# Eight query tiles of an input projection multiplied as four pairs of seven products, and decoding that begins behind them

## The chip, the cores and the metric

The kernel runs on one core of a Trainium2 chip. The metric is the device time of one launch in microseconds, the median of several runs. A profiled execution gives the rows below; its span runs from the first to the last instruction of the core.

## What is computed

One layer of a decoder step for a prompt of 512 tokens and 8 sample tokens of eight other sequences, which share one pass (520 columns, `TOK`). The hidden size is 2048. Cut to its core:

```python
h = rms_norm(x)
z = h @ w_in                       # 2048 x 7168, fp32; columns qd kd vd gd qw kw vw gw qm gm
od = differential_attention(qd, kd, vd)   # 4 heads, two 128-wide q/k halves each, value 256
ow = dilated_window_attention(qw, kw, vw) # 4 heads of 128
mk, mv = rms_norm(mem) @ w_mem_kv         # 256 memory tokens
om = attention(qm, mk, mv)                # 4 heads of 128
y = x + concat(rms(od) * silu(gd), ow * silu(gw), om * silu(gm)) @ w_out
return rms_norm(y), new keys and values
```

The sample tokens attend to caches: per sequence 1024 past keys and values of the differential heads in pages of 128 (a page table names them), a window cache and 256 memory keys and values. This is "decoding" below.

## The kernel before

**Tiles.** The output features are cut into tiles of 128 (`tiles`, L108): 8 of the memory projection (`mk`, `mv`), then 56 of the input projection: `qd` (8: head and half), per head `kd`, `vd`, `gd` (two each), `qm` (4), `qw` (4), `kw` (4), `vw`/`gw` (8), `gm` (4), and last the output projection `y`. A tile is computed transposed: the weight block is stationary, the 520 token columns move, as two halves of 260 (`HALF`) into two banks of PSUM tensor `z[0]` or `z[1]`, in turn by unit. fp32 products are made of three passes: weights and tokens are both split into a high part (`w_hi`, `act_hi`, fp32r) and a low rest (`w_lo`, `act_lo`), and hi*hi, hi*lo, lo*hi are summed. ScalarE makes `w_hi` (`split_hi`, L1351), VectorE `w_lo` (`split_lo`, L1676).

**Slots.** All engines run through one list `PLAN` of slots. A slot holds one operation on TensorE: a quarter of a single tile (`quarter`, L1097: 4 row blocks x 3 passes x 2 column halves = 24 matmuls), or half a product of a pair (`product`, L1123: 12 matmuls). Splits are made three slots ahead (`AHEAD`) in a ring of four (`SPLIT_RING`); raw weights come by SyncE's queue, 256 KB each, into a ring of eight (`WIN_RING`, L828). Behind its operation a slot has jobs that every engine does in a fixed order of rank: evacuations, turning transposes, attention steps and decoding.

**Pairs.** Ten of the sixteen `y` tiles are computed in five pairs: two tiles and the whole of the tokens make a 2x2 block product (rows of weights `A`, columns and depth of tokens `B`), with seven products in place of eight (`PRODUCTS`). It needs sums of weights (`weight_sum`, L1692 to L1700, eight a pair), sums of products (`part_copy` on ScalarE, `part_out` on VectorE, L1714 to L1729), and four operands T1 to T4 made once of the right-hand side (`operand_add`, four subtractions of 260 columns per row block; `operand_hi`, L1430 and `operand_lo`, L1757, each over 1040 columns). The operands lie in `arena`, the memory that keys, gates, pages and attention buffers use before; the raw sums lie in the places of T3's and T4's parts until these are split.

**Attention** steps (`att_steps`) come in the order scores on TensorE (A), row maximum on VectorE (`step_max`, L1797, L1804), exponential on ScalarE, normalised probabilities on VectorE (`step_probs`, L1822), turning (L1183), values, and for differential heads `o_nat` scaled on VectorE behind GpSimd's reciprocal root (L1829) and turned (L1210), gated into `cat`. Per differential head four steps, six slots apart (four in the last head).

**Decoding.** Query rows of the samples are stored to DRAM and read back broadcast (`qrows`, `q_bc`). Then 320 page units, 160 of keys (four multiply-and-add reductions each, L1865) and 160 of values (L1892, L1894), are placed in slots by the planner. It gives each slot a room of 1.5 x its length less VectorE's planned load, sums the rooms between `first` and `end`, and fills the slots in proportion:

```python
first, end = DONE[AT["qd", 1, 1]] + 4, DONE[AT["gw", 3, 0]] - 2
room = [max(0.3, 1.5 * span[s] - load[s]) for s in range(n_slots)]
```

Pages are loaded by SyncE's queue up to three slots ahead into a ring of six (`PAGE_RING`). `IN_START` is slot 32, `IN_END` slot 256. Behind the last input tile `cat` is complete, is split into `act_hi` and `act_lo` (L1596, L2144), and then its space is used for the residual (`nat`, L981).

## Time and profile before

| | |
|---|---|
| time, median of 3 runs | 1026.35 us (1026.08 to 1027.72) |
| the profiled execution | 1026.25 us |
| its span | 1024.5 us |
| TensorE matmuls busy | 98% of the span |
| weight loads busy | 96% |
| VectorE busy | 71% |
| ScalarE busy | 43% |
| GpSimd busy | 5% |
| from HBM and to it | 197 GB/s over the span |
| granted TensorE clock | 0.997 of full |

Busy shares are means over stages with different limits: preparation of tokens (to about 75 us), query tiles without decoding (to about 133), input tiles with attention and decoding (to about 771), the last input tiles, and the output projection. An engine's line in the rows gives the source line of this kernel.

### The profile page before, as it was taken

What the parts mean: (1) busy time and instruction counts of PE and PEld (TensorE: products, weight loads), DVE (VectorE), ACT (ScalarE), POOL (GpSimd) and SP (SyncE); (2) the same over time, 40 slices, a digit from 0 to 9 for tenths busy, and PEclk for the clock granted to TensorE, in tenths of its full rate; (3) what the DMA queues carried; (4) which work ended last, traced back from release to release, by engine and by line L of the source; (5) the groups of instructions that cost most, each with busy time, mean ns of one, the idle gap of its engine ahead of it and who ended that gap; (6) DMA issues with size and microseconds to landing.
All of it is one profiled execution on the core that took longest, in us unless ns stands there. A gap on an engine that the chain in (4) does not pass through costs nothing.

```text
span 1024.5 us, 24055 instructions
## 1 busy us (share of the span) xinstructions
PE 1000.5 (98%) x8103; PEld 980.4 (96%) x8103; DVE 723.7 (71%) x2687; ACT 441.5 (43%) x1169; POOL 54.7 (5%) x122
## 2 busy tenths in 40 slices
PE   7999999999999999999999999999999999999995
PEld 6899999999999999999999999999999999999995
DVE  5783267777788867778777676577774786588874
ACT  5763222222333333444342553335565365545552
POOL 0200000000000000000000000000000100000002
PEclk9999999999999999999999999999999999999998
DMA  9863288987978877777866686999662425234424
GB/s 300 250 195 107 64 266 265 293 271 226 266 220 254 259 231 235 219 224 207 245 200 192 186 249 181 231 280 284 193 191 72 140 74 153 94 104 145 124 84 167
DMA packets 254521, 203.33 MB, mean 198 GB/s; under 512 B 12480, under 2 KB 207670, under 8 KB 253750
## 3 DMA queue, kind: packets, MB, share of 16 engines
q1 hardware_dynamic: 253934, 200.67, 65.7%
q8 instruction: 65, 1.06, 0.4%
q10 hardware_dynamic: 464, 1.12, 0.3%
q14 instruction: 58, 0.48, 0.1%
HBM read 189.98 MB, written 11.76 MB: 197 GB/s over the span
## 4 chain that ended last, share of the span: by engine, by line
PE 91%; DVE 2%; ACT 2%; issue 2%; SPq 1%; DMA 1%; POOL 0%; DVEq 0%; POOLq 0%; ACTq 0%
PE z L1097 71%; PE z L1123 8%; PE o_ps L1193 2%; PE s_ps L1156 2%; PE t_ps L1143 2%; PE t_ps L1183 1%; PE s_ps L1161 1%; DMA w_raw<-in_w_mem_kv_dram 1%; PE o_ps L1198 1%; PE o_ps L1202 1%; PE s_ps L1168 1%; PE o_ps L1242 1%; ACT w_hi L1351 1%; PE s_ps L1028 1%; SPq L828 1%
## 5 line engine op out<-in xcount | busy, mean ns | idle before, releaser
L1097 PE MATMUL z<-act_hi,w_hi 128*128 128x260 f32 (+1 forms) x2048 | 440.9, 291 | 2.4 <-DVE act_lo L1629 2.3
L1097 PE MATMUL z<-act_hi,w_lo 128*128 128x260 f32 (+1 forms) x2048 | 422.4, 283 | 0.0
L1097 PE MATMUL z<-act_lo,w_hi 128*128 128x260 f32 (+1 forms) x2048 | 421.6, 282 | 0.0
L1097 PEld LDWEIGHTS z<-act_hi,w_hi 128*128 128x128 f32 x2048 | 321.5, 189 | 7.9 <-issue 4.0
L1097 PEld LDWEIGHTS z<-act_lo,w_hi 128*128 128x128 f32 x2048 | 319.9, 188 | 0.0
L1097 PEld LDWEIGHTS z<-act_hi,w_lo 128*128 128x128 f32 x2048 | 319.5, 188 | 0.0
L1676 DVE TENSOR_TENSOR w_lo<-w_raw,w_hi 128x512 fp32r<-128x512 f32 x302 | 206.8, 687 | 132.5 <-ACT w_hi L1351 131.8
L1351 ACT ACTIVATE w_hi<-w_raw 128x512 fp32r<-128x512 f32 x302 | 186.4, 626 | 200.4 <-PE z L1097 173.2
L1865 DVE CUSTOM_DVE_ANT_0 pages<-pages,q_bc 128x128 f32<-128x128 f32 x640 | 144.2, 285 | 21.2 <-DMA pages<-in_cache_k_win_dram 13.5
L1894 DVE SCALAR_TENSOR_TENSOR v_acc<-pages,dec_a,v_acc 128x256 f32<-128x256 f32 x224 | 94.3, 478 | 1.7 <-DMA pages<-in_cache_v_diff_dram 1.5
L1473 ACT ACTIVATE probs<-probs,st_n 128x128 f32<-128x128 f32 (+3 forms) x48 | 26.8, 558 | 79.9 <-DVE st_n L1804 79.6
L1865 DVE DVE_READ_ACCUMULATOR2_ANT dec_s<- 128x1 f32 x640 | 51.6, 81 | 0.0
L1491 ACT ACTIVATE probs_T<-t_ps 128x512 f32<-128x512 f32 (+3 forms) x40 | 18.8, 470 | 68.4 <-PE t_ps L1183 55.8
L1797 DVE CUSTOM_DVE_ANT_0 probs<-s_ps,bias 128x128 f32<-128x128 f32 (+3 forms) x48 | 22.3, 490 | 35.3 <-PE s_ps L1156 22.7
L1123 PE MATMUL z<-t_hi,w_hi 128*128 128x260 f32 x160 | 45.8, 286 | 0.0
L1123 PE MATMUL z<-t_hi,w_lo 128*128 128x260 f32 x160 | 45.2, 282 | 0.0
L1123 PE MATMUL z<-t_lo,w_hi 128*128 128x260 f32 x160 | 45.1, 282 | 0.0
L1351 ACT ACTIVATE w_hi<-w_sum 128x512 fp32r<-128x512 f32 x40 | 25.2, 629 | 34.2 <-DVE w_sum L1700 12.9
L1676 DVE TENSOR_TENSOR w_lo<-w_sum,w_hi 128x512 fp32r<-128x512 f32 x40 | 27.5, 687 | 14.9 <-ACT w_hi L1351 14.9
L1123 PE MATMUL z<-act_hi,w_hi 128*128 128x260 f32 x120 | 34.8, 290 | 0.5 <-DVE w_lo L1676 0.4
L1123 PE MATMUL z<-act_lo,w_hi 128*128 128x260 f32 x120 | 33.9, 282 | 0.0
L1123 PE MATMUL z<-act_hi,w_lo 128*128 128x260 f32 x120 | 33.9, 282 | 0.0
(236 smaller groups left out, 1121.8 us busy)
## 6 DMA issues: line engine op xcount, KB each, us to landing
w_raw<-in_w_in_dram SPq DMA_DIRECT2D x224, 256.0 KB, 4.5
pages<-in_cache_k_diff_dram SPq DMA_DIRECT2D x128, 256.0 KB, 4.7
pages<-in_cache_v_diff_dram SPq DMA_DIRECT2D x128, 256.0 KB, 3.6
w_raw<-in_w_out_dram SPq DMA_DIRECT2D x64, 256.0 KB, 2.8
w_raw<-in_w_mem_kv_dram SPq DMA_DIRECT2D x32, 256.0 KB, 6.1
cat<-in_x_prompt_dram SPq DMA_DIRECT2D x8, 1024.0 KB, 6.0
q_bc<-q_rows_dram SPq DMA_DIRECT2D x32, 256.0 KB, 6.7
pages<-in_cache_mem_k_dram SPq DMA_DIRECT2D x16, 256.0 KB, 6.4
```

The lines of the kernel that those rows point to most:

```text
L1097: last = nc.tensor.matmul(zb[:, bank, 0:b - a], lhs[:, w], rhs[:, kt, a:b], start=(kt == 0 and m == 0), stop=(kt == KT - 1 and m == 2))
L1123: last = nc.tensor.matmul(out, lhs[:, w], rhs[:, j, :], start=(i == 0 and j == 0 and m == 0), stop=(i == 1 and j == 3 and m == 2))
L1143: last = nc.tensor.transpose(t_ps[:, b * P:(b + 1) * P], src[:, b * P:(b + 1) * P], ident[:, :])
L1156: last = nc.tensor.matmul(s_ps[:, c, 0:(i + 1) * P], cat_t[:, 2 * h + c, i * P:(i + 1) * P], kT_t[:, key_slot("kd", h, c), 0:(i + 1) * P], ...
L1193: last = nc.tensor.matmul(o_ps[:, 0:2 * P], probs_T[:, kb * P:(kb + 1) * P], v_nat[:, h % 2, kb, :], start=(kb == 0), stop=(kb == i))
L1351: nc.scalar.activation(hi, raw, ACT.Copy).then_inc(s_hi, 1)
L1473: last = nc.scalar.activation(probs[:, c, 0:w], src, ACT.Exp, bias=st_n[:, t % 2, c:c + 1], scale=SCALE, accum_out=st_l[:, t % 2, c:c + 1])
L1491: nc.scalar.activation(probs_T[:, 0:w], t_ps[:, 0:w], ACT.Copy).then_inc(s_tfree, 1)
L1676: nc.vector.tensor_tensor(lo, raw, hi.bitcast(F32), ALU.subtract).then_inc(s_lo, 1)
L1797: last = nc.vector.tensor_tensor_reduce(probs[:, c, 0:w], s_ps[:, c, 0:w], bias[:, bi % 2, SEQ - w:SEQ], 1.0, LOWEST, ALU.add, ALU.max, st ...
L1865: last = nc.vector.tensor_tensor_reduce(seg, seg, q_bc[:, i % 2, k * P:(k + 1) * P], 1.0, 0.0, ALU.mult, ALU.add, s3[:, t, col:col + 1])
L1894: last = nc.vector.scalar_tensor_tensor(acc[:, seg], pages[:, slot, seg], a, acc[:, seg], ALU.mult, ALU.add)
```

## The change

The order of input tiles becomes: four `qm` tiles, each single as before; then the eight `qd` tiles as four pairs by the seven products; then everything else as before, without the `qm` tiles in the middle. `FIRST_QM = 4` takes all of them.

- The right-hand side of these pairs is the normalised tokens. They exist only as high and low parts, so `token_sum` adds them into `x_full` (16 additions of 520 columns), and `operand_add`, `operand_hi` and `operand_lo` make T1 to T4 of it during the `qm` tiles (`X_SUM_AT`, `X_ADD_AT`, `X_SPLIT_AT`). The same functions make the second set for the output pairs, now wholly behind `IN_END` (`T_ADDS`, `T_SPLIT_AT`).
- The parts of a query pair go straight into the query rows of `cat`.
- The operands lie in `arena` and the weight sums in the memory of the kept sample columns. So the bias tables, the kept query columns (`keep_first`), the query rows and the first pages wait for `Q_END`, the end of the fourth pair. Pages may be planned from `Q_END + 4` to two slots behind the last `gw` tile.
- Weight loads for the pairs are issued one slot behind the freeing of their place, in place of four.

`IN_END` becomes 280. Cut diff (renamed waits of equal meaning left out):

```diff
...
+FIRST_QM = 4
...
-    out += [("qd", h, c) for h in range(H) for c in range(2)]
+    out += [("qm", j, 0) for j in range(FIRST_QM)] + [("qd", h, c) for h in range(H) for c in range(2)]
...
-    out += [("qm", j, 0) for j in range(H)] + [("qw", j, 0) for j in range(H)] + [("kw", j, 0) for j in range(H)]
+    out += [("qm", j, 0) for j in range(FIRST_QM, H)] + [("qw", j, 0) for j in range(H)] + [("kw", j, 0) for j in range(H)]
...
-FIRST_IN = AT["qd", 0, 0]
+FIRST_IN = 2 * H
...
-        paired = kind == "y" and c == 0 and FIRST_PAIRED <= e <= LAST_PAIRED
+        paired = kind == "qd" or kind == "y" and c == 0 and FIRST_PAIRED <= e <= LAST_PAIRED
...
+Q_PAIRS = H
+Q_END = START[PAIRS_OF_TILES[Q_PAIRS - 1]] + 14
...
-            loads.append((n, r, slot, used[slot], event, at + (1 if first >= IN_END else AHEAD + 1)))
+            loads.append((n, r, slot, used[slot], event, at + (1 if first >= IN_END or IN_START + 8 <= first < Q_END else AHEAD + 1)))
...
-T_ADDS = ((2, -11), (0, -10), (1, -9), (4, -8), (5, -7), (3, -4), (6, 1), (7, 1))
+T_ADDS = ((2, 1), (0, 1), (1, 2), (4, 2), (5, 3), (3, 3), (6, 4), (7, 4))
 T_SPLITS = ((2, 0), (1, 0), (2, 1), (1, 1), (3, 0), (3, 1), (4, 0), (4, 1))
-T_SPLIT_AT = (-4, 2, 2, 3, 4, 4, 6, 8)
+T_SPLIT_AT = (5, 6, 7, 8, 9, 10, 11, 12)
 HEADS_AT = ((0, 1, 2, 3), (4, 5, 6, 7), (8, 9, 10, 11), (12, 13, 14), (15,))
-RESIDUAL_AT = (3, 20, 46, 74)
+RESIDUAL_AT = (5, 20, 46, 74)
+X_SUM_AT = tuple(IN_START + 1 + j // 2 for j in range(HALF_KT))
+X_ADD_AT = tuple(IN_START + 5 + 3 * j // 4 for j in range(HALF_KT))
+X_SPLIT_AT = tuple(IN_START + 11 + j for j in range(HALF_KT))
...
-    put(DONE[AT["qd", 1, 1]] + 1, "qrows", 0)
-    put(DONE[AT["qd", 3, 1]] + 1, "qrows", 1)
-    put(DONE[AT["qm", 3, 0]] + 1, "qrows", 2)
+    put(Q_END + 1, "qrows", 0)
+    put(Q_END + 2, "qrows", 1)
+    put(max(Q_END + 6, DONE[AT["qm", 3, 0]] + 1), "qrows", 2)
...
-    queries = {0: AT["qd", 1, 1], 1: AT["qd", 3, 1], WINDOW: AT["qw", 3, 0], MEMORY: AT["qm", 3, 0]}
+    ready = {0: Q_END + 4, 1: Q_END + 5, WINDOW: DONE[AT["qw", 3, 0]] + 4, MEMORY: max(Q_END + 9, DONE[AT["qm", 3, 0]] + 4)}
...
-    first, end = DONE[AT["qd", 1, 1]] + 4, DONE[AT["gw", 3, 0]] - 2
+    first, end = Q_END + 4, DONE[AT["gw", 3, 0]] + 2
...
-    assert STEPS[-1][3] + 3 < IN_END - 4 and fin0 + 5 < IN_END - 10
+    assert STEPS[-1][3] + 3 < IN_END - 4 and fin0 + 5 < IN_END - 4
     for j, (kt, turn) in enumerate(T_ADDS):
-        put(IN_END + turn, "T", ("add", j))
+        put(X_SUM_AT[j], "T", ("sum", j))
+        put(X_ADD_AT[j], "T", ("add", j))
+        put(IN_END + turn, "T", ("add", HALF_KT + j))
     for j in range(len(T_SPLITS)):
-        put(IN_END + T_SPLIT_AT[j], "T", ("split", j))
+        put(X_SPLIT_AT[j], "T", ("split", j))
+        put(IN_END + T_SPLIT_AT[j], "T", ("split", len(T_SPLITS) + j))
...
+        x_full = nc.alloc_sbuf_tensor_at("x_full", [P, HALF_KT, 2, TOK], F32, offset=base)
...
-                if s in (30, 31):
-                    bias_table(s - 30)
+                if s in (Q_END + 1, Q_END + 2):
+                    if s == Q_END + 1:
+                        sp.wait_ge(s_quarter, Q_END)
+                    bias_table(s - Q_END - 1)
...
-                        sp.wait_ge(s_tadd, len(T_ADDS))
+                        sp.wait_ge(s_tadd, 2 * len(T_ADDS))
...
-                    if k == 0:
-                        pe.wait_ge(s_tlo, T_SPLITS.index((t, i)) + 1)
+                    if k in (0, Q_PAIRS):
+                        pe.wait_ge(s_tlo, len(T_SPLITS) * (k // Q_PAIRS) + T_SPLITS.index((t, i)) + 1)
...
-                if k == 0:
-                    act.wait_ge(s_kout, 16 * len(NAT_K))
-                else:
+                if k in (0, Q_PAIRS):
+                    act.wait_ge(s_kout, 16 * (H if k == 0 else len(NAT_K)))
+                if k:
...
-                t, half = T_SPLITS[j]
-                if j == 0:
+                again, i = divmod(j, len(T_SPLITS))
+                t, half = T_SPLITS[i]
+                if j == len(T_SPLITS):
...
-                act.wait_ge(s_tadd, T_ADDED[half])
+                act.wait_ge(s_tadd, HALF_KT + T_ADDED[half] if again else HALF_KT)
                 if t >= 3:
-                    act.wait_ge(s_tlo, T_SPLITS.index((t - 2 if t == 3 else 2, half)) + 1)
+                    act.wait_ge(s_tlo, len(T_SPLITS) * again + T_SPLITS.index((t - 2 if t == 3 else 2, half)) + 1)
...
+                    if i == H:
+                        act.wait_ge(s_pdve, 7 * Q_PAIRS)
...
+                below, above = slice(0, HALF), slice(HALF, TOK)
+                queries = k < Q_PAIRS
+                if queries:
+                    row1, row2 = (cat_t[:, cat_slot(*TILES[n]), :] for n in (first, second))
+                else:
+                    row1, row2 = tall[:, 0, :], tall[:, 1, :]
...
-                    wait_tall(dve, first)
-                    nc.vector.tensor_tensor(tall[:, 0, 0:HALF], out, c1, ALU.add).then_inc(s_pdve, 1)
+                    if not queries:
+                        wait_tall(dve, first)
+                    nc.vector.tensor_tensor(row1[:, below], out, c1, ALU.add).then_inc(s_pdve, 1)
...
-                    wait_tall(dve, second)
-                    nc.vector.tensor_tensor(tall[:, 1, HALF:TOK], out, U, ALU.add).then_inc(s_pdve, 1)
+                    if not queries:
+                        wait_tall(dve, second)
+                    nc.vector.tensor_tensor(row2[:, above], out, U, ALU.add).then_inc(s_pdve, 1)
                 if name == "C12":
-                    nc.vector.tensor_tensor(tall[:, 0, HALF:TOK], out, X, ALU.add).then_inc(s_pdve, 1)
+                    nc.vector.tensor_tensor(row1[:, above], out, X, ALU.add).then_inc(s_pdve, 1)
                 if name == "C21":
-                    nc.vector.tensor_tensor(tall[:, 1, 0:HALF], out, U, ALU.add).then_inc(s_pdve, 1)
+                    nc.vector.tensor_tensor(row2[:, below], out, U, ALU.add).then_inc(s_pdve, 1)
+            def token_sum(j):
+                dve.wait_ge(s_plo, 3 * N_PREP)
+                dve.wait_ge(s_xsl, 1)
+                for i in range(2):
+                    kt = HALF_KT * i + j
+                    last = nc.vector.tensor_tensor(x_full[:, j, i, :], act_hi[:, kt, :].bitcast(F32), act_lo[:, kt, :].bitcast(F32), ALU.add)
+                last.then_inc(s_xfull, 1)
...
-                kt = T_ADDS[j][0]
-                if j == 0:
-                    dve.wait_ge(s_fin, 3)
-                if kt < H:
-                    dve.wait_ge(s_ofree, USE["C", LAST_STEP["dil", kt]]["ob"] + 1)
-                if kt >= 6:
-                    dve.wait_ge(s_ofull, USE["C", LAST_STEP["dil", 3]]["ob"] + 1)
-                b11, b12 = cat_t[:, kt, 0:HALF], cat_t[:, kt, HALF:TOK]
-                b21, b22 = cat_t[:, HALF_KT + kt, 0:HALF], cat_t[:, HALF_KT + kt, HALF:TOK]
+                if j < HALF_KT:
+                    kt = j
+                    upper, lower = x_full[:, kt, 0, :], x_full[:, kt, 1, :]
+                    dve.wait_ge(s_xfull, kt + 1)
+                else:
+                    kt = T_ADDS[j - HALF_KT][0]
+                    upper, lower = cat_t[:, kt, :], cat_t[:, HALF_KT + kt, :]
+                    if j == HALF_KT:
+                        dve.wait_ge(s_fin, 3)
+                    if kt < H:
+                        dve.wait_ge(s_ofree, USE["C", LAST_STEP["dil", kt]]["ob"] + 1)
+                    if kt >= 6:
+                        dve.wait_ge(s_ofull, USE["C", LAST_STEP["dil", 3]]["ob"] + 1)
+                    if kt >= H:
+                        dve.wait_ge(s_gated, kt - H + 1)
+                b11, b12, b21, b22 = upper[:, 0:HALF], upper[:, HALF:TOK], lower[:, 0:HALF], lower[:, HALF:TOK]
                 t1, t2, t3, t4 = (t_raw[t][:, kt, :] for t in (1, 2, 3, 4))
-                if kt >= H:
-                    dve.wait_ge(s_gated, kt - H + 1)
...
+            def keep_first():
+                pool.wait_ge(s_lo, Q_END)
+                if FIRST_QM:
+                    for j in range(FIRST_QM):
+                        wait_tile(pool, AT["qm", j, 0])
+                    nc.gpsimd.tensor_copy(q_s[:, 3 * H:3 * H + FIRST_QM, :], cat_t[:, 3 * H:3 * H + FIRST_QM, SAMPLE]).then_inc(s_keep, FIRST_QM)
+                wait_tile(pool, AT["qd", H - 1, 1])
+                nc.gpsimd.tensor_copy(q_s[:, 0:2 * H, :], cat_t[:, 0:2 * H, SAMPLE]).then_inc(s_keep, 2 * H)
...
-                    elif kind == "evac" and TILES[what] in KEPT:
+                    elif kind == "evac" and TILES[what] in KEPT and DONE[what] > Q_END:
                         keep(what)
+                    elif (kind, what) == ("part", (Q_PAIRS - 1, "C21")):
+                        keep_first()
...
```

## Rows read from the trace of the kernel before

**Rows 1.** Busy time of TensorE over the span, share, instructions.

```profile
PE 1000.5 (98%) x8103; PEld 980.4 (96%) x8103; DVE 723.7 (71%) x2687; ACT 441.5 (43%) x1169; POOL 54.7 (5%) x122
```

**Rows 2.** What TensorE waited for: us in total, times, longest.

```profile
PE t_ps L1247 <- DMA rows<-in_g_mem_norm_dram: 5.4, 1, 5.4
PE z L1097 <- DVE act_lo L1629: 2.3, 3, 1.0
```

**Rows 3.** The chain in order of time: start us, us, what.

```profile
83.06 43.24 PE z L1097 x360
...
919.02 11.52 PE z L1123 x96
```

**Rows 4.** Stretches: us, busy us of each engine, granted clock, DMA share, GB/s.

```profile
75.00:133.00 58.00, 58.00 (x487) 57.99 (x486) 16.09 (x28) 16.62 (x31) 1.17 (x4) 1.00 0.35 99
...
296.00:375.00 79.00, 79.00 (x626) 76.59 (x625) 65.46 (x405) 26.12 (x60) 4.87 (x14) 1.00 0.79 241
...
881.00:988.00 107.00, 106.50 (x886) 105.96 (x885) 88.91 (x162) 59.20 (x163) 4.96 (x9) 1.00 0.39 117
```

**Rows 5.** VectorE in order of time: start us, us, line, operation.

```profile
840.71 2.52 DVE L2144 TENSOR_TENSOR act_lo<-cat,act_hi 128x520 fp32r<-128x520 f32 x4
...
843.76 0.42 DVE L1745 TENSOR_TENSOR t_raw<-cat 128x260 f32<-128x260 f32 x1
...
845.24 0.42 DVE L1745 TENSOR_TENSOR t_raw<-cat 128x260 f32<-128x260 f32 x1
...
847.42 2.39 DVE L1757 TENSOR_TENSOR t_lo<-t_raw,t_hi 128x1040 fp32r<-128x1040 f32 x2
```

**Rows 6.** ScalarE's groups from 840 to 872 us: busy us, mean ns.

```profile
L1430 ACT ACTIVATE t_hi<-t_raw 128x1040 fp32r<-128x1040 f32 x7 | 7.4, 1063 | 4.1 <-DVE t_raw L1750 3.8 <-DVE t_lo L1757 0.3
```

**Rows 7.** Timeline of VectorE and TensorE at two places.

```profile
121.37 0.69 DVE L1676 TENSOR_TENSOR w_lo<-w_raw,w_hi 128x512 fp32r<-128x512 f32 x1 [2.18 <-ACT w_hi L1351]
...
129.12 0.40 PE L1097 MATMUL z<-act_hi,w_hi 128*128 128x260 f32 x2
...
677.05 0.69 DVE L1676 TENSOR_TENSOR w_lo<-w_raw,w_hi 128x512 fp32r<-128x512 f32 x1
...
679.40 0.49 PE L1097 MATMUL z<-act_hi,w_hi 128*128 128x260 f32 x2
```

**Rows 8.** VectorE's groups from 881 to 988 us, the output pairs.

```profile
L1692 DVE TENSOR_TENSOR w_sum<-w_raw 128x512 f32<-128x512 f32 x9 | 6.2, 685 | 0.0
...
L1725 DVE TENSOR_TENSOR tall<-z,k_nat 128x260 f32<-128x260 f32 x5 | 2.1, 430 | 0.5
```

**Rows 9.** VectorE's groups from 296 to 375 us.

```profile
L1865 DVE CUSTOM_DVE_ANT_0 pages<-pages,q_bc 128x128 f32<-128x128 f32 x160 | 35.7, 284 | 0.4 <-DMA pages<-in_cache_k_diff_dram 0.4
...
L1865 DVE DVE_READ_ACCUMULATOR2_ANT dec_s<- 128x1 f32 x160 | 12.8, 80 | 0.0
```

**Rows 10.** Timeline of one differential step of three key blocks.

```profile
374.38 0.62 DVE L1822 SCALAR_TENSOR_TENSOR probs<-probs,st_r 128x384 f32<-128x384 f32 x1
...
375.35 0.49 PE L1183 MATMUL t_ps<-ident,probs 128*128 128x128 f32 x3
```

**Rows 11.** Stretches, as in rows 4.

```profile
173.00:233.00 60.00, 60.00 (x503) 60.00 (x503) 43.56 (x294) 17.51 (x30) 1.26 (x5) 1.00 0.91 288
183.00:193.00 10.00, 10.00 (x86) 10.00 (x85) 7.24 (x54) 2.87 (x5) 0.29 (x1) 1.00 0.97 304
650.00:680.00 30.00, 30.00 (x254) 30.00 (x253) 15.92 (x93) 8.60 (x16) 0.75 (x3) 1.00 1.00 251
```

**Rows 12.** DMA issues over the span: times, KB each, median us to landing.

```profile
w_raw<-in_w_in_dram SPq DMA_DIRECT2D x224, 256.0 KB, 4.5
pages<-in_cache_k_diff_dram SPq DMA_DIRECT2D x128, 256.0 KB, 4.7
...
q_bc<-q_rows_dram SPq DMA_DIRECT2D x32, 256.0 KB, 6.7
```

**Rows 13.** What VectorE waited for from 630 to 715 us.

```profile
DVE pages L1865 <- DMA pages<-in_cache_k_win_dram: 13.5, 9, 3.1
```

33 lines of the change are left out of this document (14 added, 19 removed).

## Prediction

> **What bounds the kernel now.** I read the busy times first: TensorE's matmuls cover 98% of the span [rows 1]. Such a share can hide slack, so the second view was what TensorE waited for: the longest entries are 5.4 us for the first load and 2.3 us for `act_lo` while the tokens are prepared [rows 2]. Third, the chain in order of time: it is one run of matmuls after another. 360 matmuls of 260 columns take 43.24 us, 96 take 11.52 us, so one costs 0.120 us [rows 3]. TensorE's instruction stream sets the end, from the first slot to the last, and a matmul that is left out is worth 0.120 us wherever it stood, provided VectorE, ScalarE and the transfers keep up with the shorter stream. The rest is therefore about how much room these have.
>
> A "slot" below is one entry of the plan: a quarter of a single tile (24 matmuls, 2.88 us), or half a product of a pair (12 matmuls, 1.44 us).
>
> **What is removed.** A single tile is 4 quarters of 24 = 96 matmuls, two tiles 192. A pair is 14 halves of 12 = 168. Four pairs save 4 x 24 = 96 matmuls: 96 x 0.120 = **-11.5 us**. The matmuls of a product go at the same rate as those of a quarter (96 in 11.52 us, in both forms) [rows 3]. The four memory query tiles are only moved: nothing on TensorE.
>
> **What is added for the operands of the pairs.** All of it is VectorE and ScalarE work in the slots behind the token preparation, where VectorE was busy 16.1 of 58 us [rows 4].
> - 16 sums of 520 columns (`token_sum`). Four subtractions of 520 columns take 2.52 us, so 0.63 each [rows 5]: 10.1 us.
> - 32 subtractions of 260 columns (`operand_add`): one group of four takes 1.48 us from start to start (843.76 to 845.24) [rows 5]: 8 x 1.48 = 11.8 us.
> - 8 `operand_lo` of 1040 columns, two in 2.39 us [rows 5]: 9.6 us. ScalarE's 8 `operand_hi` are 1.06 us each [rows 6].
>
> That is 31.5 us, and beside it go the weight splits of these 18 slots at about 0.6 us each, 10.8 us: 42 us in the 52 us of those slots. The densest place before the pairs is the first four slots, 2.52 + 0.6 = 3.1 us of work per 2.88 us: 1 us is lost against TensorE, while low halves are ready 7.0 us ahead here (a `w_lo` ends at 122.06, its quarter begins at 129.12) [rows 7]. Cost nothing; without that lead it would be 1 us. The last three of the eight splits fall into slots of 1.44 us, where VectorE then has 0.6 (weights) + 0.6 (weight sum) + 1.2 = 2.4 us to do. It falls 2.9 us behind over three slots, and a product slot gives it at most three slots, 4.3 us, of lead. Bounds 0 and 2.9; I take **+0.8 us**, nearer the low end, since the lead nearly covers it.
>
> **The four pairs themselves.** Per pair VectorE has 14 splits and 8 weight sums (685 ns as recorded, about 0.6 from start to start, since they overlap a little) and 7 parts (430 ns, about 0.35) [rows 8]: 22 x 0.6 + 7 x 0.35 = 15.7 us in 20.2 us. The output pairs carry the same and `y_add`, `times_g` besides: 88.9 of 107 us, and TensorE was without a matmul for only 0.5 us in five pairs [rows 4]. So the query pairs are the lighter kind: four fifths of 0.5, **+0.4 us** (bounds 0 and 1.5).
>
> **Decoding begins later.** Before, cache pages could be planned from slot 52 to slot 238, 186 slots. After, `Q_END` is 32 + 16 + 56 = 104 and the window is 108 to 266, 158 slots: the 12 query slots, the 16 slots of the memory queries and 4 for the delay are gone at the front, 4 are won at the end. The same 320 pages go into it. The planner spreads them by room, 1.5 x length - load. Summed by its own formula the room is 680.9 before and 585.6 after (I moved the slots' loads), so every slot gets **1.163 times** the pages. What that does:
>
> *VectorE beside attention.* Between 296 and 375 us it is busy 65.5 of 79 us, the densest stretch I found [rows 4]. 160 segments of key pages with their accumulator reads are 35.7 + 12.8 = 48.5 us of it [rows 9], 1.21 us a page. 0.163 x 48.5 = 7.9 us more gives 73.4 of 79, 93%. It still fits. But the hand-overs are tight: in the third step of each of the four differential heads the probabilities are ready only 0.35 to 0.46 us before TensorE turns them (one stands: 374.38 + 0.62 = 375.00 against 375.35) [rows 10]. Between the row maximum and the probabilities lie the pages of one slot, 2.1 before by the formula, 2.4 after: 0.34 page x 1.21 = 0.4 us, all of the margin. As pages are whole, perhaps one in three of these steps gets a page more and stalls 0.8 us: 4 x 0.8 / 3 = 1.1, halved for the two heads whose steps lie beside cheaper value pages, 0.7. With somewhat more than as much again for the second hand-over of a step (`o_nat`), where VectorE's pages stand ahead in the same way, I take **+1.6 us**. Bounds: 0, and 12.8 us if each of the eight steps beside key pages stalls 0.8 us at both.
>
> *Transfers of the first keys.* From 173 to 233 us 288 GB/s move on the mean at a share of 0.91, and in the stretch from 183 to 193 us 304 at 0.97 [rows 11]. A slot of 2.88 us carries one 256 KB weight block, 1.69 pages of 256 KB and an eighth of a `q_bc` per page [rows 12]; 16.3% more of the latter two is 0.081 MB, or 28 GB/s: 316, about what a share of 1.00 would give by these rows (304 / 0.97 = 313, 288 / 0.91 = 316). For 22 slots, 63 us, against 308, 2.5% less than that and the lowest I would read into them, the deficit is 1.6 us, against the 7.0 us lead of the splits: nothing, bounds 0 and 1.6. The Trainium skill (DMA: Bandwidth & Descriptors, Specifications) gives an HBM limit of about 358 GB/s per core. By that figure 316 would be no bound and this upper end would be 0; the trace shows full shares well below it, at 251 GB/s in one stretch, so I keep the bound from the rows.
>
> *Transfers of the window keys.* This is the weakest place. Between 650 and 680 us the share is 1.00 at 251 GB/s [rows 11], VectorE waited 13.5 us in nine waits for `in_cache_k_win`, and the lead of the splits fell from 7 us to 1.7 us (a `w_lo` ends at 677.74, its quarter begins at 679.40) [rows 7, 13]. After, the 16 pages are planned over 11 slots in place of 13, with fewer key tiles stored beside them and the memory steps stretching the first slots. Transfers: 4.2 MB of pages, 2.1 of `q_bc`, 2.9 of weights, about 0.5 of stores, 9.7 MB at 250 GB/s = 39 us for slots worth 34 us, against 10.75 MB, 43 us, for 39 us before: 5 us behind in place of 4. The lead left was 1.7: **+1.2 us**; bounds 0 and 5.
>
> **The second set of operands moves behind `IN_END`.** All eight `operand_add` come in four slots now: 2 x 1.48 + 0.6 = 3.6 us of work per 2.88. Over the slots IN_END + 1 to + 4 VectorE loses some 3 us, where it was already at its tightest behind the `act_lo` blocks (2.52 us each) [rows 5]. Splits go first in each slot. **+1.0 us**, bounds 0 and 3. The residual's load waits for these on SyncE's queue with weight loads behind it; these are issued ten slots ahead, so nothing. The same for SyncE's wait for `Q_END` before the bias tables: eight weight blocks are in flight by then.
>
> **The sum.** -11.5 + 0.8 + 0.4 + 1.6 + 1.2 + 1.0 = -6.5 us. The profiled execution took 1026.25 us (span 1024.5 and 1.75 around it), so 1019.75; the runs' median is 0.1 above it, 1026.35: **1019.9 us**.
>
> **Rivals.**
> - *Everything is hidden* (0.20): the leads of 7 us absorb all of it, -11.5: 1014.9 us. For it: TensorE hardly waits anywhere now. Against: three places with under 2 us of margin.
> - *The transfers become the bound* (0.18): full share in the first keys (1.6) and the whole of 5 us lost at the window keys, with the rest as above: -11.5 + 1.2 + 1.6 + 1.6 + 5 + 1.0 = -1.1 us: 1025.2 us. For it: the full shares. Against: weights are asked for eight slots ahead, and only they stop TensorE at once.
> - *VectorE becomes the bound beside attention* (0.15), the one that ends slower: the 93% is an average, VectorE's queue is in order, and each `step_max`, `step_probs` and `o_nat` stands behind pages. At its bound of 12.8 us the sum is -11.5 + 1.2 + 12.8 + 1.2 + 1.0 = +4.7: 1031.1 us. It decides from 8.1 us on (11.5 - 3.4), that is when each of the 16 differential steps costs TensorE more than 0.5 us.
> - The forecast has 0.47.
>
> **How the numbers follow.** About 0.2% (2 us) is what a measurement of this kernel can tell from no change. Faster than that: the forecast, all hidden, and 0.07 of the transfer case, 0.74. Within it: 0.11 of the transfer case and 0.02 of the VectorE case, 0.13. Slower: 0.13. The range goes from just under all hidden, 1014.4, to 1026.4, behind the transfer case; what is left out is mostly the slower case. The forecast's own range is 1017 to 1023.
>
> **What the profile of the changed kernel would show.** 96 fewer matmuls: on the quarters' line each of the three kinds goes from 2048 to 1792, on the products' line the total from 840 to 1512. A query pair of 20.2 us in the chain. VectorE near 93% in the stretch beside the first two heads, with its waits for `s_ps` gone; that it stays under 90% would speak for "all hidden". DMA share at 1.0 behind the fourth pair. If TensorE's waits name `probs` or `o_nat` with over 8 us, the slower rival is right; if they name `w_lo` while VectorE waits for pages, the transfers are. The prediction is wrong altogether if a pair does not run at 0.120 us per matmul, or if the shorter window pushes the end of decoding into the slots before `IN_END`, where `cat` has to be complete.

## The result and the profile after

The changed kernel takes **1043.21 us** (median of 4 runs, 1043.14 to 1043.79) against 1026.55 us for the kernel before on the same chip: ratio 1.0162, 95% interval 1.0144 to 1.0179, 16.7 us slower. Forecast were 1019.9 us, 6.5 us faster, and a range that ended at 1026.4. The profiled execution has a span of 1041.1 us against 1024.5.

Busy time of the changed kernel, which answers to [rows 1], and the costliest group of matmuls of each of the two lines:

```profile
PE 998.0 (96%) x8007; PEld 972.9 (93%) x8007; DVE 796.0 (76%) x2827; ACT 460.5 (44%) x1197; POOL 55.7 (5%) x112
```

```profile
L1114 PE MATMUL z<-act_hi,w_hi 128*128 128x260 f32 (+1 forms) x1792 | 390.2, 293 | 3.5 <-DVE act_lo L1647 1.9
...
L1140 PE MATMUL z<-t_hi,w_hi 128*128 128x260 f32 x288 | 82.2, 285 | 0.3 <-DVE w_lo L1694 0.2
```

The work is what was forecast: 8103 - 8007 = 96 matmuls fewer, 1792 on each kind of a quarter. But TensorE is busy 96% in place of 98%, and VectorE 72 us longer. What TensorE waited for from 205 to 850 us (us in total, times, longest), where before no wait was over 0.8 us:

```profile
PE t_ps L1225 <- DVE o_nat L1870: 4.1, 3, 2.9
PE t_ps L1198 <- DVE probs L1863: 2.8, 1, 2.8
PE o_ps L1257 <- DVE o_nat L1870: 1.7, 1, 1.7
PE t_ps L1257 <- ACT rows L1586: 1.5, 1, 1.5
PE z L1114 <- DVE w_lo L1694: 1.5, 1, 1.5
PE t_ps L1198 <- ACT v_nat L1471: 1.4, 1, 1.4
```

The stretches of the four pairs, the first keys and the attention beside them (columns as in [rows 4]):

```profile
121.00:204.00 83.00, 81.95 (x673) 80.91 (x671) 67.64 (x118) 38.38 (x64) 0.21 (x1) 1.00 0.35 102
204.00:277.00 73.00, 71.56 (x597) 71.24 (x595) 45.84 (x297) 19.82 (x36) 1.46 (x6) 1.00 0.80 243
277.00:350.00 73.00, 69.16 (x542) 67.36 (x543) 63.31 (x426) 22.83 (x53) 3.71 (x11) 0.98 0.89 278
350.00:437.00 87.00, 83.10 (x656) 80.14 (x655) 74.71 (x480) 27.76 (x65) 5.00 (x14) 1.00 0.85 258
```

VectorE is at 87% beside attention, under the 93% forecast, and the DMA share is 0.80 to 0.89, within what it was before (0.79 to 0.91 [rows 4, 11]). No engine is full, and yet TensorE stalls: these averages don't show where the time went.

**An account of TensorE's time.** For each run I took every matmul of the trace, in order, and counted it at the median distance from its start to the next start that its kind has in that run; the sum is "work", and what the clock shows beyond it is "lost". (Attention and decoding matmuls count too.) Lost us by stretch, each bounded by the start of the tile named:

| stretch | before | changed | late start, singles (f1) | both light (f2) | keys spread (j1) | two pairs, placed (j2) |
|---|---|---|---|---|---|---|
| to `qd` 0 | 9.4 | 10.2 | 8.9 | 9.3 | 9.8 | 9.4 |
| `qd` 0 to `kd` 0 | 0.3 | 2.6 | 0.3 | 2.4 | 2.5 | 2.6 |
| `kd` 0 to `kd` 2 (first keys) | 2.6 | 10.1 | 2.5 | 3.6 | 2.9 | 2.7 |
| `kd` 2 to `qw` 0 (attention) | 6.4 | 12.8 | 16.8 | 9.8 | 10.5 | 6.2 |
| `qw` 0 to `vw` 0 | 6.2 | 7.0 | 6.6 | 5.0 | 8.7 | 6.5 |
| `vw` 0 to `y` 0 | 3.5 | 11.6 | 14.8 | 8.6 | 18.9 | 8.1 |
| output tiles | 2.9 | 5.6 | 3.3 | 5.8 | 6.0 | 2.4 |
| lost in all | 31.3 | 59.9 | 53.2 | 44.5 | 59.3 | 37.9 |
| work | 970.6 | 958.7 | 967.5 | 958.7 | 959.1 | 964.5 |

The change takes away 11.9 us of work and adds 28.6 us of lost time, together the 16.7 us. Thirteen separate stalls of 0.7 to 3.0 us between 205 and 840 us are some 20 us of it. The account is good to about 3 us: f1 has exactly the matmuls of the kernel before, and its "work" still comes out 3.1 us lower, so its 53.2 is too high by about that. Single runs of the changed kernel's variants scatter by up to 4.8 us around their medians.

**One stall followed back.** VectorE of the changed kernel before TensorE's stall of 3.0 us at 292 us (start us, us):

```profile
284.30 0.69 DVE L1815 SCALAR_TENSOR_TENSOR gate<-gate,z 128x520 f32<-128x520 f32 x1
287.22 0.29 DVE L1904 CUSTOM_DVE_ANT_0 pages<-pages,q_bc 128x128 f32<-128x128 f32 x1 [2.23 <-DMA pages<-in_cache_k_diff_dram]
...
290.99 0.28 DVE L1838 CUSTOM_DVE_ANT_0 probs<-s_ps,bias 128x128 f32<-128x128 f32 x1
...
293.34 0.69 DVE L1694 TENSOR_TENSOR w_lo<-w_raw,w_hi 128x512 fp32r<-128x512 f32 x1
...
294.58 0.35 DVE L1863 SCALAR_TENSOR_TENSOR probs<-probs,st_r 128x128 f32<-128x128 f32 x1
```

TensorE's matmuls on both sides of the stall, and what VectorE waited for from 230 to 295 us:

```profile
291.75 0.41 PE L1114 MATMUL z<-act_hi,w_lo 128*128 128x260 f32 x2
294.99 0.48 PE L1198 MATMUL t_ps<-ident,probs 128*128 128x128 f32 x1 [2.83 <-DVE probs L1863]
```

```profile
DVE pages L1904 <- DMA pages<-in_cache_k_diff_dram: 18.1, 13, 4.1
```

A key page lands 2.2 us late. Behind it on VectorE's queue stand two more pages, two weight splits and `step_max` (290.99); behind that ScalarE's exponential, then two further pages and a split on VectorE, `probs` at 294.58, and the turn that TensorE waits for. The wait is on TensorE's list under `probs`; a late page and the pages that stand ahead of each hand-over make it up together. What SyncE issued before that page:

```profile
279.27 0.45 SPq L862 DMA_DIRECT2D q_bc<-q_rows_dram  x1
280.50 1.48 SPq L873 DMA_DIRECT2D pages<-in_cache_k_diff_dram  x2
```

The page is the first of a new row of samples, right behind that row's `q_bc` (256 KB). This is where VectorE waits most: of its 19.4 us of waits for the 44 key pages issued from 215 to 295 us, 15.3 us are at the six pages right behind a `q_bc`, which take 6.1 to 7.3 us to land, the others 4.6 on the median.

### The profile page after: what moved, and what is told of

Read it like the earlier page. It is cut to its first block and busy times, and to the rows that moved or that the text cites. A ratio compares the mean times of both kernels' runs of the same rounds, so it can differ in the third digit from the quotient of the medians.

```text
span 1041.1 us, 24166 instructions
## 1 busy us (share of the span) xinstructions
PE 998.0 (96%) x8007; PEld 972.9 (93%) x8007; DVE 796.0 (76%) x2827; ACT 460.5 (44%) x1197; POOL 55.7 (5%) x112
## 5 line engine op out<-in xcount | busy, mean ns | idle before, releaser
L1114 PE MATMUL z<-act_hi,w_hi 128*128 128x260 f32 (+1 forms) x1792 | 390.2, 293 | 3.5 <-DVE act_lo L1647 1.9
L1114 PE MATMUL z<-act_hi,w_lo 128*128 128x260 f32 (+1 forms) x1792 | 371.8, 283 | 0.0
L1114 PE MATMUL z<-act_lo,w_hi 128*128 128x260 f32 (+1 forms) x1792 | 371.2, 283 | 0.0
L1114 PEld LDWEIGHTS z<-act_hi,w_hi 128*128 128x128 f32 x1792 | 283.4, 189 | 9.1 <-issue 4.1
L1114 PEld LDWEIGHTS z<-act_lo,w_hi 128*128 128x128 f32 x1792 | 281.6, 189 | 0.0
L1114 PEld LDWEIGHTS z<-act_hi,w_lo 128*128 128x128 f32 x1792 | 281.2, 189 | 0.0
L1140 PE MATMUL z<-t_hi,w_hi 128*128 128x260 f32 x288 | 82.2, 285 | 0.3 <-DVE w_lo L1694 0.2
L1140 PEld LDWEIGHTS z<-t_hi,w_hi 128*128 128x128 f32 x288 | 54.1, 188 | 0.8 <-DVE w_lo L1694 0.7
L1140 PEld LDWEIGHTS z<-t_hi,w_lo 128*128 128x128 f32 x288 | 54.2, 188 | 0.0
L1140 PEld LDWEIGHTS z<-t_lo,w_hi 128*128 128x128 f32 x288 | 54.1, 188 | 0.0
```

Of the source, the lines that this page charges most:

```text
L1114: last = nc.tensor.matmul(zb[:, bank, 0:b - a], lhs[:, w], rhs[:, kt, a:b], start=(kt == 0 and m == 0), stop=(kt == KT - 1 and m == 2))
L1140: last = nc.tensor.matmul(out, lhs[:, w], rhs[:, j, :], start=(i == 0 and j == 0 and m == 0), stop=(i == 1 and j == 3 and m == 2))
```

## The experiments

Two theories stood first: A, the shorter window crowds VectorE's pages beside attention, so that hand-overs to TensorE come late; and P, the loss comes with the pairs and their order. Transfers were the third. Later ones (D for the density of the window, O for the order, V, J, T, H, B, L, W) are named where they come in.

### What costs the time: order, length of the window, or the pages

**e1_late_singles.** No pairs, `qm` tiles first, the decode window as short as in the changed kernel, second operands as there:

```diff
-    out += [("qd", h, c) for h in range(H) for c in range(2)]
+    out += [("qm", j, 0) for j in range(H)] + [("qd", h, c) for h in range(H) for c in range(2)]
...
-    first, end = DONE[AT["qd", 1, 1]] + 4, DONE[AT["gw", 3, 0]] - 2
+    first, end = DONE[AT["qd", 3, 1]] + 4, DONE[AT["gw", 3, 0]] + 2
```

> No query pair: the four memory query tiles and then the eight differential ones are all multiplied singly, as in the kernel before; but pages are planned from four slots behind the last query tile to two behind the last gw tile (158 slots, summed room 585.6, as in the changed kernel), and the second operands are made behind IN_END as there. Theory A (the later start squeezes decoding, VectorE's queue falls late beside attention): the 28.2 us that the changed kernel lost, less some 2.9 of its query stage, come without any pair, 1026.5 + 25 = 1051 us, 1047 to 1055. Rival P (the pairs and their operands cost the time): 1027, within 2 us.

Measured 1045.87 us, ratio 1.0193 (1.0159 to 1.0226). Just under the 1047 to 1055 of theory A, and far from P's 1027.

**e2_memory_queries_first.** The first half of that edit alone: `qm` first, single tiles, the window from slot 68 to 238, room 625.3.

> Only the order of the tiles: memory queries first, no pair, pages from four slots behind the fourth differential query tile as before (170 slots, summed room 625.3, 1.09 times the pages of before in a slot). Theory A: a part of the loss, in proportion or less, 1029 to 1038 us. Rival O (the order itself, with the memory steps no longer beside memory query tiles, costs the time): nearly as much as with the late start. Rival P: 1027.

Measured 1036.15 us, ratio 1.0098 (1.0068 to 1.0128): already half of e1's loss, within theory A's range. But more than half of it falls between `qw` 0 and `vw` 0, with the longest stall, 3.5 us, at 539 us; there the changed kernel loses only 0.8 us more than the kernel before. So e2 isn't simply a milder form of the same loss, and a share of the order in it is not excluded.

**f1_before_late_start.** The order of before, nothing but a later start:

```diff
-    first, end = DONE[AT["qd", 1, 1]] + 4, DONE[AT["gw", 3, 0]] - 2
+    first, end = DONE[AT["qd", 1, 1]] + 4 + 28, DONE[AT["gw", 3, 0]] - 2
```

> The kernel before with one edit: decoding may begin at slot 80 in place of 52, tile order and single tiles as before. The planner's room falls from 680.9 to 583.6, about the changed kernel's 585.6. Theory D (what the changed kernel lost comes from the same pages in a shorter window): the late singles with that room took 1045.9, so this takes 1040 to 1050. Rival O (it comes from where the new tile order puts the memory tiles and steps beside each other, the window matters little): under 1033, within 6 us of before.

Measured **1045.48 us**, ratio 1.0189 (1.0165 to 1.0213). One line of the kernel before, and 19 us are gone. It has neither pairs nor the new order: a late start alone costs as much as the whole change. With 680.9, 625.3 and 585 of room the lost time is 31, 44 and 50 to 53 us (before, e2, e1 and f1). The place differs, though: in the first keys f1 loses no more than the kernel before (2.5 us against 2.6), the changed kernel 10.1. Its loss there needs more than the shorter window, and what more isn't shown.

**e3_light_pages.** The changed kernel with light arithmetic on the pages:

```diff
-                    seg = pages[:, slot, k * P:(k + 1) * P]
+                    seg = pages[:, slot, k * P:k * P + 16]
...
-                for k in range(n):
+                for k in range(n if t == 0 else n // 2):
```

It leaves out 7/8 of each key multiplication, and half of the additions of each value page behind a sample's first.

> The changed kernel with light page arithmetic: keys multiply 16 of the 128 columns of a head, values behind the first page of a row add only half of the columns; all transfers and waits stay. Theory A (VectorE's time): the loss behind the query stage goes, 1026.5 - 11.5 + 2.9 = 1018 us, 1016 to 1021. Rival T (the transfers are the bound): over 1034 us, since every transfer stays. If both matter it lies between.

Measured 1036.79 us, ratio 1.0104 (1.0075 to 1.0133): 6 us better than the changed kernel, not 25. VectorE still waits 30.4 us in 25 waits for key pages from 205 to 300 us. Its load is a part, and not the larger one.

**e4_half_page_transfers.** The changed kernel; pages of the differential heads load 64 of 128 rows from the seventh on, so the computation uses stale rows for the rest:

```diff
-                dst = pages[:, slot, :]
+                full = seq < PAGE_RING or g >= WINDOW
+                rows_ = P if full else P // 2
+                dst = pages[0:rows_, slot, :]
...
```

> The changed kernel with half the bytes of the differential pages (64 of 128 rows from the seventh page on, so the arithmetic reads old rows); all arithmetic stays. Rival T (transfers are the bound): 1018 to 1024 us. Theory A: VectorE's waits for pages go (31 us of them), which gives back the lead of the splits at the first keys and some 3 to 6 us of TensorE's time, 1036 to 1041 us.

Measured 1056.17 us, ratio 1.0293 (1.0239 to 1.0347): slower than whole pages, and outside both expectations. The median time to landing is 4.6 us for 128 KB from 230 to 290 us, against 4.8 for the whole page, so this run doesn't test what a faster landing would give. Why it is slower still stays open.

**f2_both_light and f3_before_both_light.** The arithmetic of e3, and 128 of 512 columns of each page (64 KB), on the changed kernel and on the kernel before:

```diff
-                dst = pages[:, slot, :]
+                cut = P if seq >= PAGE_RING and g < WINDOW else None
+                dst = pages[:, slot, 0:cut]
...
```

> The changed kernel with both loads of the pages cut at once: keys multiply 16 of 128 columns, values past the first page add half of the columns, and pages of the differential heads from the seventh on transfer 128 of 512 columns. What the output needs of the decode part is left out; the instructions and their order are the same. The light arithmetic alone gave 1036.8. Theory V (VectorE and the transfers each hide behind the other): 1017 to 1024. Rival J (the collisions of jobs in a slot, which stay): above 1030.

> The kernel before with the same two cuts as the both-light run, as its control; the same part of the computation is left out. Before hardly waits, so both theories expect 1022 to 1026. The difference of the two runs is what pairs and order give when the pages cost little: -11.5 plus 2.9 for the query stage by theory V, about +5 by rival J.

Measured 1028.07 us, ratio 1.0010 (1.0000 to 1.0020), and 1027.56 us, ratio 1.0002 (0.9993 to 1.0012). Neither theory's number, and the control is 1.6 us above its range too: 15 us come back, the pairs' gain doesn't. Some stalls are left with light pages: those of the changed kernel at 470, 530 and 795 us stand here at 460, 520 and 779. Jobs that share a slot and pass one PSUM bank (h2 shows it for the first), or stand one behind the other on a queue, would do that. The light run has 11.7 us more lost time than its control (44.5 against 32.8).

### Issue and landing in the first keys

What the bytes alone give, f2 shows against e3, which has the same light arithmetic: 1036.79 - 1028.07 = 8.7 us. From 205 to 300 us TensorE's matmuls are busy 90.7 of 95 us in the changed kernel, 92.2 in e3 and 95.0 in f2. So a page's bytes do count.

In the light run VectorE waits for key pages as long as in the changed kernel, though a page is a quarter as large, lands in 2.9 us and the DMA share is 0.64. Rows of the light run: waits from 230 to 295 us, issues from 230 to 290 us.

```profile
DVE pages L1905 <- DMA pages<-in_cache_k_diff_dram: 18.6, 15, 3.5
```

```profile
pages<-in_cache_k_diff_dram SPq DMA_DIRECT2D x38, 64.0 KB, 2.9
```

The light arithmetic hides the gain there, since VectorE is free sooner: e3 waits 30.4 us from 205 to 300 us, f2 20.0. And each `q_bc` in the light run is still 256 KB. Landing is one half of a page's delay; the other is its issue. Issues of the changed kernel from 230 to 290 us (times, KB, median us to landing), and SyncE's queue in order of time:

```profile
pages<-in_cache_k_diff_dram SPq DMA_DIRECT2D x36, 256.0 KB, 4.8
w_raw<-in_w_in_dram SPq DMA_DIRECT2D x19, 256.0 KB, 4.8
q_bc<-q_rows_dram SPq DMA_DIRECT2D x4, 256.0 KB, 7.3
```

```profile
244.86 1.48 SPq L873 DMA_DIRECT2D pages<-in_cache_k_diff_dram  x2
246.38 0.66 SPq L843 DMA_DIRECT2D w_raw<-in_w_in_dram  x1
247.81 1.45 SPq L873 DMA_DIRECT2D pages<-in_cache_k_diff_dram  x2
249.30 0.43 SPq L843 DMA_DIRECT2D w_raw<-in_w_in_dram  x1
250.49 1.60 SPq L873 DMA_DIRECT2D pages<-in_cache_k_diff_dram  x2
```

Two pages start 1.13 us apart: each needs its number from the page table in a register (a load of 0.27 us, with the address arithmetic 0.7) and 0.34 us to issue. A plain transfer takes 0.49. The 36 pages and 27 other transfers of these 60 us are 36 x 1.13 + 27 x 0.49 = 53.9 us; 4.3 us are waits for buffers, and under 2 us are left. A slot of 2.88 us has room for a weight block (0.49), its part of the queries and stores (8 in 21 slots, 0.19) and 2.20 / 1.13 = **1.95 pages**. Before, the plan asked for 1.69 a slot and 35 came in 60 us (170 to 230); the changed kernel's asks for two in nearly every slot, and 36 come. The Trainium skill (Trainium Kernel Development and Optimization, Key Constraints) says that issuing from several engines only saves the sequencer's issue time; by these rows that time is nearly used up here. Issuing pages from a second queue was not tried.

Followed page by page, over the first 80 us of decoding (us; medians, but for the waits):

| run | pages | from free buffer to issue | from issue to landing | VectorE's waits | of these right behind a `q_bc` |
|---|---|---|---|---|---|
| before | 46 | 1.7 | 5.6 | 4.4 | 1.7 |
| changed | 44 | 4.1 | 4.9 | 19.4 | 15.3 |
| e3, light arithmetic | 44 | 4.6 | 4.9 | 31.3 | 19.3 |
| f2, quarter pages too | 47 | 5.2 | 2.9 | 19.5 | 14.1 |
| j1, below | 41 | 2.8 | 5.4 | 8.3 | 8.3 |

Against the kernel before, landing is no slower; pages are issued 2.4 us later. That speaks for SyncE's queue, whose time per page has no term in the forecast. It is not proof: the queue of the kernel before was as busy (35 pages and 30 other transfers from 170 to 230 us), and the light run's is later still, yet with a landing 2 us shorter TensorE stays busy. Queue and landing add up, and no run changes the queue alone. Asking for a row's `q_bc` earlier, where most of the wait is, was not tried either.

**j1_first_keys_spread.** The changed kernel with fewer pages in the first slots:

```diff
+    for s in range(first, first + 24):
+        room[s] *= 0.8
     total = sum(room[first:end])
```

> The changed kernel; the planner's room in the first 24 slots of the decode window is multiplied by 0.8, so that the key pages come there at about the rate of the kernel before, and the rest of the window takes them. Theory T (the first key pages come late, VectorE waits for one with step_max behind it, and TensorE stalls at 275 and 292 us): these two stalls, 4.7 us, and the half clock behind them go, and some come back later as the rest is denser: 1037 to 1041. Rival (VectorE's load is the limit, the transfer only the last to arrive): the stalls stay or move, 1043 or more.

Measured 1043.83 us, ratio 1.0171 (1.0140 to 1.0202). The mechanism of the expectation holds, with the rival's number: VectorE's waits for the first keys fall from 19.7 to 10.3 us, both stalls are gone, and at `qw` 0 the run has lost 25.7 us in place of 35.7. But 9.4 us are lost again later, most of it in the first tiles behind `vw` 0: from 653 to 694 us this run loses some 11 us, the changed kernel in the 41 us from the same tile on some 3. Fewer pages are fewer bytes and fewer issues at once, so j1 doesn't tell the two apart. Rows of this run there: VectorE, TensorE, SyncE, and the granted clock (third column from the right) of 653 to 694 us.

```profile
677.09 0.28 DVE L1906 CUSTOM_DVE_ANT_0 pages<-pages,q_bc 128x128 f32<-128x128 f32 x1
682.11 0.29 DVE L1906 CUSTOM_DVE_ANT_0 pages<-pages,q_bc 128x128 f32<-128x128 f32 x1 [4.73 <-DMA pages<-in_cache_k_win_dram]
...
683.57 0.42 DVE L1881 COPY cat<-o_ps 128x256 f32<-128x256 f32 x1
```

```profile
684.13 0.61 PE L1249 MATMUL o_ps<-dc,ones 128*128 128x32 f32 x2 [3.39 <-DVE cat L1881]
```

```profile
667.52 0.63 SPq L889 DMA_DIRECT2D pages<-in_cache_k_win_dram  x1
675.11 0.38 SPq L864 DMA_DIRECT2D q_bc<-q_rows_dram  x1
```

```profile
653.00:694.00 41.00, 35.19 (x252) 33.63 (x251) 26.04 (x116) 15.62 (x47) 1.60 (x2) 0.92 0.74 200
```

The same chain with another head: SyncE stands 7 us at `q_bc`, of which there are two buffers, until VectorE has done the keys of the row two before; the next window page is behind it on SyncE's queue and lands 4.7 us late; behind that page on VectorE's queue is the copy of a PSUM bank that TensorE needs. The clock of 0.92 is 0.08 x 41 = 3.3 us of the loss.

**k1_seven_page_buffers and k2_two_pairs_seven_buffers.** `PAGE_RING = 7`, with `dec_a` and `o_nat` moved to other memory, on the changed kernel and on h4 (below).

> The changed kernel with seven page buffers in place of six (two small tensors move to make room); the same work in the same slots. Theory L (a page is asked for too late, since its buffer comes free too late): VectorE's waits for key pages up to 300 us, 19.7 us with six, fall by a third or more, the stalls at 275 and 292 us shrink, 1036 to 1040. Theory W (the transfers' bandwidth): the waits stay, 1042 to 1045.

> Two pairs with the third page behind o_nat and the sums moved (1.0003 of before) and seven page buffers. Theory L: 1 to 3 us faster, 1024 to 1026.5, the first version ahead of the kernel before. Theory W: 1027 to 1028.

Measured 1043.11 us, ratio 1.0149 (1.0129 to 1.0168), and 1027.17 us, ratio 1.0006 (0.9997 to 1.0016). VectorE's waits up to 300 us are 21.2 us in place of 19.7. Theory L falls: with pages already issued 4.1 us behind a free buffer, one buffer more changes nothing. Theory W's numbers came, but a slow queue gives the same, so they don't decide between the two.

### Hand-overs and shared banks

**h1_third_page_behind.** In a slot with the output of a differential step, VectorE takes pages ahead of `o_nat`; here the third goes behind it:

```diff
-        for kind, what in sorted(jobs, key=lambda j: rank.get(j[0], 6)):
+        ahead = [j for j in jobs if j[0] in ("dk", "dv")][:2]
+        place = lambda j: 4.5 if waits and j[0] in ("dk", "dv") and j not in ahead else rank.get(j[0], 6)
+        for kind, what in sorted(jobs, key=place):
```

> The changed kernel; where a slot holds the output of a differential step and three pages, VectorE takes the third page behind o_nat in place of ahead of it. Nothing else moves. TensorE's stalls at the turn of o_nat behind three-page slots were 1.1, 3.0 and 1.2 us (345, 371 and 410 us). Theory H (a page that stands ahead of a hand-over in VectorE's queue is what stalls TensorE): 4 to 7 us faster than the changed kernel, 1036 to 1039. Rival (the hand-over waits for GpSimd's squares or for VectorE's mean load): within 1.5 us of 1043.2.

Measured 1040.61 us, ratio 1.0113 (1.0092 to 1.0135). Between the two expectations. The ratio is 0.5% under that of the changed kernel, yet the profiled execution shows little of it: the stall at 372 us fell from 3.0 to 2.0, that at 410 went, that at 346 stayed. The direction holds, the size is not settled.

**h2_sums_moved and h3_both_moved.** Turns of value sums (`do`) leave slots that hold the output of a differential step or the turn of a new key or value; h3 has both edits.

```diff
-                summed[g, 2 * p + j] = s + j + (2 if g < WINDOW else 1)
+                s1 = max(s + j + (2 if g < WINDOW else 1), max(summed.values(), default=0))
+                while s1 < DONE[AT["vw", 0, 0]] and any(k == "nat" or k == "C" and STEPS[w][0] == "diff" for k, w in slots[s1]):
+                    s1 += 1
+                summed[g, 2 * p + j] = s1
```

> The changed kernel; a turn of the decoded value sums (do) that was planned into a slot with the output of a differential step or the turn of a new key or value goes one slot later. Two stalls of the changed kernel stand there (2.0 us at 470, part of 1.3 us at 745). Theory B (two jobs in one slot pass the same PSUM bank, and the second waits until the first is copied out): 2 to 4 us faster, 1039 to 1041. Rival (TensorE only waits there because VectorE is behind): no change, 1042.5 to 1044.

> The changed kernel with both edits: the third page behind o_nat and the value sums moved. If the stalls are independent, the gains add: 1032 to 1037. If VectorE's load is the limit, the stall only moves to a later hand-over: above 1040.

Measured 1045.22 us, ratio 1.0165 (1.0147 to 1.0183), and 1042.42 us, ratio 1.0151 (1.0133 to 1.0168). h2 is slower than either expectation has it, h3 is in its second, "above 1040". The stall of 2.0 us at 470 is gone, as theory B has it, and new ones stand at 504 (1.75) and 754 (2.1). The edit has traded one stall for others.

### Fewer pairs

**f4_two_pairs.** Heads 0 and 1 alone as pairs, decoding from slot 80 (the first group's queries are then complete):

```diff
-        paired = kind == "qd" or kind == "y" and c == 0 and FIRST_PAIRED <= e <= LAST_PAIRED
+        paired = kind == "qd" and e < 2 or kind == "y" and c == 0 and FIRST_PAIRED <= e <= LAST_PAIRED
...
-Q_PAIRS = H
+Q_PAIRS = 2
```

> The changed kernel with only heads 0 and 1 as pairs; heads 2 and 3 are single tiles again, and decoding begins at slot 80, behind the second pair. 48 matmuls fewer than before (-5.8 us), room 641.2 of the planner against 585.6 with four pairs and 680.9 before. By theory D the loss goes with the room (9.6 us at 625.3, 19.3 us at 585.6 with single tiles), so 6 us here: 1026.5 - 5.8 + 0.6 + 6 = 1027, range 1023 to 1031. By rival O the loss is that of the order, 17 us and more: 1035 to 1040.

Measured 1029.80 us, ratio 1.0032 (1.0019 to 1.0044), near the 1027 of theory D.

**h4_two_pairs_moved and j2_two_pairs_placed.** h4 adds the edits of h1 and h2; j2 moves in addition every softmax step and sum before the window keys out of slots where another job passes the same bank.

> Two pairs (1029.8) with the same two edits. In its trace the turn of a value sum waits 2.0 us at 465, 1.7 at 498 and 1.1 at 739; there is no stall at o_nat. Theories H and B: 1026 to 1028. Rival: 1029 to 1031.

> Two pairs, third page behind o_nat, and every value sum and softmax step before the window keys moved out of slots in which another job passes the same PSUM bank. The version with the first two edits took 1.0003 of before, with stalls of 1.75 us at 495 and 1.1 at 643 left. Theory B: both go, 1024 to 1026, faster than before. Rival: they come back elsewhere, 1027 to 1029.

Measured 1027.72 us, ratio 1.0003 (0.9993 to 1.0012), and 1027.41 us, ratio 1.0008 (0.9998 to 1.0018). With a looser window the first two edits do pay, 0.3% or 3 us: the stall of f4 at 465 us is gone (1.9 us), the one of 1.75 stays. The further moves take that one away too, and the time stays where it was, the rival's number.

**j3_four_pairs_placed and j4_before_placed.** All edits with four pairs (keys spread too), and the edits on the kernel before as the control.

> Four pairs with all three edits: third page behind o_nat, sums and softmax steps moved, first keys spread. If the causes are separate and each is mended, 1030 to 1034; if the window of 158 slots is simply too dense, not under 1036. In neither case as fast as two pairs.

> The kernel before with the same placement edits (third page behind o_nat, sums and softmax steps moved), as the control. Its trace shows two stalls of 0.9 us that these edits don't touch. Both theories: within 2 us of before.

Measured 1038.33 us, ratio 1.0097 (1.0078 to 1.0116), and 1027.04 us, ratio 1.0000 (0.9990 to 1.0009). The best of four pairs is 10 us behind, not under the 1036 that was set for a window simply too dense; the edits give the kernel before nothing, which has only two stalls of 0.9 us that they don't touch. No version tried beats the kernel before.

## Why the prediction was wrong

- **What is removed, -11.5.** Right: 96 matmuls, 11.9 us of work by the account.
- **Operands of the pairs +0.8, four pairs +0.4.** 1.2 forecast; up to `kd` 0 the changed kernel loses 12.8 us against 9.7, so 3.1, inside the bounds (0 to 4.4).
- **Decoding begins later.** The room of 585.6 and the factor 1.163 were right; the price was not. A late start alone, f1, costs 1045.48 - 1026.66 = 18.8 us, where the forecast had 2.8 for the three places that follow. The changed kernel loses 22.8 us in them.
- **Transfers of the first keys, 0 with bounds 0 and 1.6: the step that failed first.** It set 316 GB/s against what a full share moves, and let a late page cost only what the lead of the splits didn't cover; but `step_max` has no such lead and stands behind the page. The stretch from `kd` 0 to `kd` 2 loses 7.5 us more. Mean bandwidth was the wrong measure: the share there was 0.89, and 353 GB/s moved from 298 to 304 us, yet single pages came up to 4.1 us late. The density of pages is what costs (j1), buffers are not (k1). The forecast had no term for the issue of a page, 1.13 us on SyncE's queue with two asked for in 2.88 us, nor for the landing of a page right behind a `q_bc`. How the 7.5 us divide between these is open.
- **VectorE beside attention, +1.6, bounds 0 and 12.8.** From `kd` 2 to `qw` 0: +6.4 us. VectorE reached 87%, not 93, so the mean load was even overestimated. The size was off because it was made of hand-overs that slip by 0.8 us; they slip by 1.1 to 3.0. TensorE's waits that name `probs` and `o_nat` sum to 2.8 + 4.1 + 1.7 = 8.6 us, just over the 8 set as the mark of the slower rival. That rival had the right sign and, for pages ahead of hand-overs, the right mechanism; but 2.8 of the 8.6 stand behind a late page, 1.7 at a value sum's turn, and at 1031.1 its price was too small.
- **Transfers of the window keys, +1.2, bounds 0 and 5.** From `qw` 0 to `y` 0: +0.8 + 8.1 = 8.9 us. Here too the lead of the splits was reckoned, and not what stands behind a page on VectorE's queue or behind a `q_bc` on SyncE's. The part of this in shared banks alone isn't separated; the light run has 3.9 of it.
- **Second operands, +1.0.** The output tiles lose 2.7 us more with four pairs, but with two pairs, whose second operands come in the same four slots, 2.4 us against 2.9 before. So that move costs nothing, and the 2.7 are something else: two stalls of 1.1 and 0.9 us at 896 and 1004 us, at a copy of `tall` beside the output pairs. Their cause is open.
- **Left out altogether:** TensorE's clock behind a stall (below), and that the places are coupled: in j1 pages taken from one place are paid at another.

The sum by stretch is -11.9 + 3.1 + 7.5 + 6.4 + 8.9 + 2.7 = +16.7 us.

What is shown is that a shorter window costs this much (f1, and f4 with fewer pairs), and that TensorE's loss is in hand-overs behind late or queued pages. What stays open: the first keys, as said above, and how the loss of attention and window divides between late pages, pages ahead of hand-overs and shared banks. h1, h2 and j3 move single stalls as expected, but the totals don't add.

## What to carry to other kernels

A shared, already tuned window of filler work is a resource of its own: before moving its start, try the move alone, it is one line. Count each in-order queue as an engine, instruction by instruction with its register loads, for the densest slots and not for the mean, and see which large transfer stands right ahead of one that is waited for. And price a late transfer by what stands behind its consumer in that queue: a lead on one product (here the weight splits) protects nothing else.

## What the runs showed of the hardware

**The clock fell behind one stall, not behind another as long.** The changed kernel around its stall of 3 us, and behind the one that ends at 374.1 us (columns as in [rows 4]):

```profile
288.00:294.00 6.00, 4.16 (x35) 3.94 (x33) 5.96 (x43) 2.28 (x7) 0.00 (x0) 1.00 0.94 291
295.00:298.00 3.00, 3.00 (x14) 3.00 (x15) 3.00 (x24) 0.79 (x2) 0.00 (x0) 0.51 0.72 216
298.00:304.00 6.00, 6.00 (x50) 5.80 (x49) 4.69 (x31) 2.19 (x5) 0.97 (x2) 1.00 1.06 353
374.00:378.00 4.00, 3.85 (x33) 3.86 (x34) 3.66 (x22) 0.00 (x0) 0.00 (x0) 1.00 0.66 203
```

After 2.8 us without a matmul (292.2 to 295.0) the granted clock is 0.51 for 3 us, the lower level of 1.2 GHz, and back at 2.4 GHz behind it: 3 x 0.49 = 1.5 us on top of the stall. After 2.9 us without one, up to 374.1, it stays at 1.00. The trace of the kernel before shows no fall between 75 and 1020 us.

**Half of the partitions was not half of a transfer's time.** 64 of 128 rows of a page (e4) landed in 4.6 us on the median, a whole page in 4.8, and the kernel was 13 us slower; 128 of 512 columns of all rows (f2) landed in 2.9.
